# Weight blocks of the first expert stage loaded ahead into the places of S5 tables

## What is computed

```python
for g in range(MOE_GROUPS):                      # 4 groups of 8 experts
    sl = slice(g * MOE_EXPERTS_PER_GROUP, (g + 1) * MOE_EXPERTS_PER_GROUP)
    hg = jnp.einsum('nd,edf->nef', x, w_gate[sl])
    hu = jnp.einsum('nd,edf->nef', x, w_up[sl])
    act = (jax.nn.silu(hg.astype(f32)) * hu.astype(f32)) * combine[:, sl, None]
    y = y + jnp.einsum('nef,efd->nd', act.astype(x.dtype), w_down[sl]).astype(f32)
```

## Time and profile before

| | us |
|---|---|
| median of 3 runs | 1056.37 |
| lowest, highest | 1055.56, 1063.42 |
| profiled execution | 1059.69 |
| its span, first to last instruction | 1057.8 |
| busy: PE, DVE, ACT, POOL | 948.3, 415.3, 197.0, 380.3 |
| mean granted TensorE clock | 0.97 of full |

### The profile page before, as it was taken

One profiled execution on the slowest core, in us unless ns is written; L12 is line 12 of the kernel. 1 busy time (PEld: TensorE's weight loads), 2 busy tenths in 40 slices (PEclk: granted clock), 3 DMA queues, 4 the chain that ended last, 5 costly groups with the idle time before them and its releaser, 6 DMA issues.

```text
span 1057.8 us, 15969 instructions
## 1 busy us (share of the span) xinstructions
PE 948.3 (90%) x5788; PEld 578.5 (55%) x5788; DVE 415.3 (39%) x918; ACT 197.0 (19%) x386; POOL 380.3 (36%) x650
## 2 busy tenths in 40 slices
PE   4999989999988878888799699999999999777896
PEld 4888878655554444444444585444456555434452
DVE  4500245686643223132227781132465233221226
ACT  5423231322300000000025531002441000000012
POOL 1278920193266666666662640000021211101000
PEclk9999999999999999899999899999989999999999
DMA  7127870651779999999983955721067999999964
GB/s 252 41 80 284 305 285 3 262 188 41 278 301 410 419 421 426 422 410 391 389 310 135 154 132 247 317 106 73 20 252 284 421 422 427 422 424 425 422 249 194
DMA packets 45924, 292.06 MB, mean 276 GB/s; under 512 B 10737, under 2 KB 12017, under 8 KB 26391
## 3 DMA queue, kind: packets, MB, share of 16 engines
q1 hardware_dynamic: 35463, 269.92, 64.8%
q0 software_dynamic: 8640, 16.03, 4.1%
q10 hardware_dynamic: 1760, 5.31, 1.7%
HBM read 270.10 MB, written 36.80 MB: 290 GB/s over the span
## 4 chain that ended last, share of the span: by engine, by line
PE 56%; DMA 24%; DVE 6%; SPq 4%; POOL 4%; issue 4%; ACT 1%; POOLq 1%; DVEq 0%; ACTq 0%
PE ps L769 13%; DMA arena<-in_w_gu 11%; PE ps L912 10%; PE ps L1069 10%; DMA arena<-in_w_down 8%; PE ps L1302 5%; PE ps L1055 3%; POOL arena L2461 3%; PE ps L986 2%; SPq L586 2%; DMA arena<-scratch_yd 2%; DVE arena L1706 2%; SPq L582 2%; PE ps L731 2%; PE ps L942 1%
## 5 line engine op out<-in xcount | busy, mean ns | idle before, releaser
L1069 PE MATMUL ps<-arena 128*64 128x256 f32 x2048 | 247.6, 400 | 38.3 <-DMA arena<-in_w_gu 38.3
L1069 PEld LDWEIGHTS ps<-arena 128*64 128x64 f32 x2048 | 154.1, 144 | 131.3 <-DMA arena<-in_w_gu 42.3
L2362 POOL TENSOR_TENSOR arena<-arena 128x32 f32<-128x32 f32 (+5 forms) x233 | 119.0, 511 | 154.6 <-DMA arena<-in_s_d 68.3
L2461 POOL TENSOR_TENSOR arena<-arena 128x256 f32<-128x256 f32 (+3 forms) x192 | 132.1, 688 | 40.5 <-POOL arena L2461 40.0
L769 PE MATMUL ps<-arena 128*128 128x256 f32 (+1 forms) x640 | 142.1, 383 | 0.3 <-ACT arena L1414 0.3
L769 PEld LDWEIGHTS ps<-arena 128*128 128x128 f32 x640 | 121.0, 190 | 19.1 <-ACT arena L1414 0.5
L1055 PE MATMUL ps<-arena 128*64 128x512 f32 x512 | 119.0, 605 | 12.2 <-DMA arena<-in_w_down 11.3
L2109 DVE TENSOR_TENSOR arena<-arena,ps 128x128 f32<-128x128 f32 x64 | 18.4, 287 | 249.0 <-ACT arena L1557 248.9
L912 PE MATMUL ps<-arena 128*128 128x512 f32 x256 | 114.6, 597 | 1.1 <-DMA arena<-in_w_out 1.0
L1557 ACT ACTIVATE arena<-ps 128x128 f32<-128x128 f32 x64 | 17.8, 278 | 460.2 <-PE ps L1069 460.2
L912 PEld LDWEIGHTS ps<-arena 128*128 128x128 f32 x256 | 47.0, 190 | 55.2 <-issue 52.9
(11 more groups left out here) (231 smaller groups left out, 1001.5 us busy)
## 6 DMA issues: line engine op xcount, KB each, us to landing
arena<-in_w_gu SPq DMA_DIRECT2D x64, 2048.0 KB, 14.0
arena<-in_w_down SPq DMA_DIRECT2D x64, 1024.0 KB, 14.0
arena<-in_w_in SPq DMA_DIRECT2D x10, 1024.0 KB, 6.4
scratch_yd<-arena SPq DMA_DIRECT2D x2, 4160.0 KB, 17.7
arena<-scratch_yd SPq DMA_DIRECT2D x16, 512.0 KB, 7.7
arena<-in_w_out SPq DMA_DIRECT2D x1, 4096.0 KB, 12.5
scratch_hd<-arena ACTq DMA_DIRECT2D x8, 512.0 KB
arena<-in_w_glu SPq DMA_DIRECT2D x2, 2048.0 KB, 7.8
```

What stands on the lines that cost most here:

```text
L1069: mm = pe.matmul(ps[CAP * f:CAP * f + CAP, 2 + s, 0:256], XT[l][:, kc, CAP * s:CAP * s + CAP], w[:, kc, 256 * f:256 * f + 256], start=kc = ...
L2362: step(g_.tensor_tensor(out, a, b, op))
L2461: g_.tensor_tensor(o, x, y, f).then_inc(sem("matrix_steps"), 1)
```

## The change

- New places: `EARLY_GU` (two gate-up blocks, at A+38824 and A+34728) and `EARLY_WD` (two sets of down blocks, at A+30632 and A+26536). They lie where GR, GI and M stand later.
- Before `experts(0)` SyncE loads eight blocks ahead or earlier than before: expert 1's gate-up behind the S5 loads; pair 0's down blocks once GpSimd has B-bar and the sample's states are stored; experts 2 and 3 once the sample's output is mixed; expert 5 and pair 2's down blocks behind `x_mixed`; pair 1's down blocks behind the last router product and `h_out`.
- In the stage the early places are filled a second time, for pairs 3 and 4. From pair 5 on the order is that of before.
- There is no S5 build in pairs 0 to 5, 14 and 15. In pairs 6 to 13 two builds are done per pair. V's part (12 tensor_tensor of 256 elements per pair) moves to VectorE (`inputs_of`), ahead of its other work of the pair; GpSimd keeps GR's and GI's (12 operations of 288 elements). TensorE does eight transposes per pair in two groups, VectorE two copies.
- Places that overlapped the new ones move (CS, DB, one of HB). The load of CS also waits for `pool_mixed`. Several semaphores are merged into others.

```diff
+        EARLY_GU = [place(A + at, KC, 512) for at in (38824, 34728)]
+        EARLY_WD = [[place(A + at + 2048 * b, 4, 512) for b in range(2)] for at in (30632, 26536)]
...
             load(DSK, T["s5_d"], "s5_in")
+            def early_gate_up(e, c):
+                sp.dma_start(EARLY_GU[c], T["w_gu"][0][e]).then_inc(sem(f"early_gu_{c}"), 16)
+
+            def early_down(p, c, b):
+                sp.dma_start(EARLY_WD[c][b], T["w_down"][0][b][p]).then_inc(sem(f"early_wd_{c}"), 16)
+
+            sp.wait_ge(sem("stored"), 16 * 4)
+            early_gate_up(1, 0)
             sp.wait_ge(sem("mlstm_parts"), 3)
...
+                    if l == 0 and isinstance(r, int):
+                        sp.wait_ge(sem("gu_done_0"), 1)
+                        load_first(0, 4, 0)
+                        for p in (0, 1):
+                            sp.wait_ge(sem("gu_done_0"), 2 * p + 2)
+                            early_gate_up(2 * p + 7, p)
+                            for b in range(2):
+                                sp.wait_ge(sem("down_done_0"), 2 * p + b + 1)
+                                early_down(p + 3, p, b)
+                            sp.wait_ge(sem("gu_done_0"), 2 * p + 3)
+                            load_first(0, 2 * p + 6, 1 - p)
+                        sp.wait_ge(sem("gu_done_0"), 6)
+                        load_gate_up(0, 11, 0, 1)
+                        for b in range(2):
+                            sp.wait_ge(sem("down_done_0"), 4 + b + 1)
+                            load_down(0, 5, 0, b)
+                        for p in (3, 4):
+                            sp.wait_ge(sem("gu_done_0"), 2 * p + 1)
+                            load_first(0, 2 * p + 4, p % 2)
+                        pair(5, 0, 1)
+                        with sp.Fori(3, 7) as k:
+                            for half in range(2):
+                                pair(2 * k + half, 0, half)
+                        pair(EP - 2, 0, 0, first=False)
...
+            sp.wait_ge(sem("s5_by_pool"), 2)
+            sp.wait_ge(sem("stored"), 16 * 7)
+            for b in range(2):
+                early_down(0, 0, b)
+            sp.wait_ge(sem("mlstm_parts"), 4)
+            load_first(0, 2, 1)
+            early_gate_up(3, 1)
             sp.wait_ge(sem("x_mixed"), 1)
+            load_gate_up(0, 5, 0, 1)
+            for b in range(2):
+                load_down(0, 2, 0, b)
             for n in range(2):
                 load(CIN[n], T["s5_cb"][n], "s5_in")
+            sp.wait_ge(sem("routed"), routed(0, "lg", 4))
+            sp.wait_ge(sem("h_out"), 80)
+            for b in range(2):
+                early_down(1, 1, b)
             experts(0)
...
+                    def inputs_of(p, h):
+
+                        q = 2 * p - 12 + h
+                        two = bass.ds(4 * p - 24 + 2 * h, 2)
+                        br_, bi_ = (a_[:, two].unsqueeze(2).broadcast_to((P, 2, L, CW)) for a_ in (BBR, BBI))
+                        pr_, pi_ = spread(BACKR[:, two], CW), spread(BACKI[:, two], CW)
+                        dve.wait_ge(sem("s5_by_pool"), 3)
+                        dve.wait_ge(sem("m_turned"), q + 1)
+                        done = 0
+                        for out, other, op in ((VR[h], (br_, bi_), ALU.subtract), (VI[h], (bi_, br_), ALU.add)):
+                            for o, x, y, f in ((out, pr_, other[0], ALU.mult), (VTMP, pi_, other[1], ALU.mult),
+                                               (out, out, VTMP, op)):
+                                done += 1
+                                v.tensor_tensor(o, x, y, f).then_inc(sem("v_steps"), 1)
+                                dve.wait_ge(sem("v_steps"), 6 * q + done)
+                        dve.sem_inc(sem("v_ready"), 1)
...
-                    pr_, pi_ = spread(BACKR[:, two], CW), spread(BACKI[:, two], CW)
-                    br_, bi_ = by_step(BBR, L), by_step(BBI, L)
-                    pool.wait_ge(sem("m_turned"), t + 1)
-                    pool.sem_inc(sem("marks"), 1)
-                    mul_add(VR[half], pr_, br_, pi_, bi_, ALU.subtract, GTMP[:, :, 0:L])
-                    mul_add(VI[half], pr_, bi_, pi_, br_, ALU.add, GTMP[:, :, 0:L])
-                    pool.sem_inc(sem("v_ready"), 1)
+                    pool.sem_inc(sem("g_ready"), 1)
```

More of the change, by code:

```diff
@@ L677, in _ @@
             ring.wait_full(sp, "zs", 1)
+            sp.wait_ge(sem("turns_in"), 16)
             load_turns(1)
@@ L1097, in turns @@
                     if l == 0:
-                        with pe.Fori(0, EP // 2 - 1) as k:
-                            for half in range(2):
-                                pair(2 * k + half, half, 0, 2 * k + half, turn=half, k=k)
+                        if isinstance(r, int):
+                            for p in range(6):
+                                pair(p, p % 2, 0, p, turn=p % 2, k=p // 2)
+                            with pe.Fori(3, 7) as k:
+                                for half in range(2):
+                                    pair(2 * k + half, half, 0, 2 * k + half, turn=half, k=k, build=True)
+                        else:
+                            with pe.Fori(0, EP // 2 - 1) as k:
+                                for half in range(2):
+                                    pair(2 * k + half, half, 0, 2 * k + half, turn=half, k=k)
                         if isinstance(r, int):
@@ L2103, in turns, with pair @@
                         lists_again(r)
-                    def pair(p, k, half, follows, last=False):
+                    def inputs_of(p, h):
[13 more added lines that the diff above has]
+                        dve.sem_inc(sem("v_ready"), 1)
+                    def pair(p, k, half, follows, last=False, build=False):
                         n = 2 * p + E * r
+                        if build:
+                            for h in range(2):
+                                inputs_of(p, h)
                         for s in range(2):
@@ L2149, in turns @@
                         ts(RK, RK, -float(CAP), None, ALU.add)
-                    for half in range(2):
-                        pair(half, 0, half, True)
-                    with dve.Fori(1, E // 4 - 1) as k:
+                    if l == 0 and isinstance(r, int):
+                        for p in range(6):
+                            pair(p, p // 2, p % 2, True)
+                        with dve.Fori(3, E // 4 - 1) as k:
+                            for half in range(2):
+                                pair(2 * k + half, k, half, True, build=True)
+                    else:
                         for half in range(2):
-                            pair(2 * k + half, k, half, True)
+                            pair(half, 0, half, True)
+                        with dve.Fori(1, E // 4 - 1) as k:
+                            for half in range(2):
+                                pair(2 * k + half, k, half, True)
                     if isinstance(r, int):
@@ L2510, in scatter, with build @@
                                               ).then_inc(sem(f"y_out_{l}_{half}"), 16)
-                    def build(p, half):
-                        if l == 0 and isinstance(r, int):
-                            matrices(p, half, p)
+                    def build(p):
+                        for h in range(2):
+                            matrices(2 * p - 12 + h)
                     if not isinstance(r, int):
@@ L2528, in turns @@
                         most_rows = pool.value_load(most[0:1, l:l + 1], min_val=0, max_val=NT)
-                    with pool.Fori(0, EP // 2 - 2) as k:
-                        for p, half in ((2 * k + 1, 1), (2 * k + 2, 0)):
-                            scatter(p - 1, 1 - half)
-                            gather(p + 2, half)
-                            build(p, half)
-                    scatter(EP - 4, 0)
-                    gather(EP - 1, 1)
-                    build(EP - 3, 1)
+                    if l == 0 and isinstance(r, int):
+                        for p in range(1, 6):
+                            scatter(p - 1, (p - 1) % 2)
+                            gather(p + 2, p % 2)
+                        with pool.Fori(3, EP // 2 - 2) as k:
+                            for half in range(2):
+                                p = 2 * k + half
+                                scatter(p - 1, 1 - half)
+                                gather(p + 2, half)
+                                build(p)
+                        scatter(EP - 5, 1)
+                        gather(EP - 2, 0)
+                        build(EP - 4)
+                        scatter(EP - 4, 0)
+                        gather(EP - 1, 1)
+                        build(EP - 3)
+                    else:
+                        with pool.Fori(0, EP // 2 - 2) as k:
+                            for p, half in ((2 * k + 1, 1), (2 * k + 2, 0)):
+                                scatter(p - 1, 1 - half)
+                                gather(p + 2, half)
```

(4 more changed lines are left out.)

156 lines of the change are left out of this document (91 added, 65 removed).

## The result

The changed kernel takes 1042.62 us (median of 4 runs, 1039.97 to 1043.31), the kernel before beside it 1057.94 (4 runs): a ratio of 0.9839, with a 95% interval of 0.9806 to 0.9871. Timed again it gave 0.983 [0.9795, 0.9865]. The forecast was 1037.2, in a range of 1029 to 1049.

A forecast was written before the change was run, and what follows sets the result against it. It took layer 0's experts to be bound by DMA bytes. Terms 20.2 + 1.0 - 1 - 1 gave 19.2 us off a median of 1056.4, so 1037.2, in a range of 1029 to 1049.

The forecast's parts named there:

- What bounds the stage: Layer 0's experts cost what their bytes cost: 16.4 us per pair at 416 GB/s; TensorE alone would need 12.0.
- the bytes ahead: Ahead of layer 0's experts, 8.39 MB more is loaded in a hole of the DMA: 20.2 us won.
- rival 3: Early loads issued only near 270, so only the hole from 290 to 297 is filled: 1050 us; chance 0.07.
- The dip near 350: After the early places' last issue the DMA may run dry for 0 to 2 us; taken as -1.
- VectorE's operations: In pairs 6 to 13, twelve of 0.42 us, 0.3 more for six meeting GpSimd: 7.3 us per pair.
- rival 1: VectorE and GpSimd in lock-step, 1.2 us per operation, 38 us lost in pairs 6 to 13: 1075 us; chance 0.07.
- The cover of 0.79 us per operation: In pairs 6 to 13, VectorE's twelve operations cost nothing up to 0.79 us each: (16.7 - 7.2) / 12.
- Theory A: Expectation for 14 VectorE operations: changed kernel at the knee, 18.9 to 19.3 us per pair, 10 to 16 us slower.
- what might get through: In pairs 6 to 13, waits for VectorE that reach the DMA's order, taken as -1 us.
- The tail: End of the stage, pairs 14 and 15 and the reads of stored rows: 0 to 1 us, taken as 0.
- the starting value: Whole kernel before the change: median 1056.4 us, from which the forecast subtracted its sum.

The follow-up runs named there:

- The loads put off: Changed kernel with all early loads issued only once x is mixed, near 270 us: 1053.72 us, 13.2 above the changed kernel beside it.
- the second profile: For the changed kernel: it was run again with no edit, 1040.53 us, stage 229.3 us.
- operations of 512: Changed kernel with VectorE's 12 build operations of 256 elements per pair merged to 6 of 512: 1042.5 us, ratio 0.9837 to the kernel before.
- the two kernels with more operations: Changed kernel with VectorE's build multiplications done twice over, for 12 operations per pair: 20 took 1096.37 us, 14 took 1061.15 us.
- VectorE's third: Changed kernel with VectorE doing 4 of its 12 build operations per pair, tables wrong: 1039.82 us, ratio 0.9832 to the kernel before.
- the filled wait: Changed kernel with 24 extra matmuls ahead of TensorE's wait for the first stored rows behind the stage: 1042.41 us, ratio 0.9852.

## Why the prediction was right

**What bounds the stage, and the bytes ahead: held.** Two profiles of each kernel give 249.1 and 248.6 us before, 230.05 and 229.3 after: 19.05 and 19.3 us for a sum of 19.2. That they agree so closely is chance, since the stages in the table above differ by 3 us. Of the things named ahead, the DMA engines are busy for 0.61 x 6 + 10.3 + 3.8 = 17.8 us from 236 to 262 (15 were expected by 256), the first five pairs are 12.0 apart (six were expected), the waits for weights begin with pair 5 (6 or 7), and the mean period from pair 5 to pair 13 is 17.1 in the one profile and 16.6 in the other (16.4 to 17). The last gate-up block is issued at 516.96, 16 us earlier than before (20 were expected). The loads put off gave 11 us back, and without them the kernel takes what rival 3 says of a head start that isn't had: 5.4 us won by the ratio, 6 in the rival.

**The dip near 350: 0 to 4 us for 1.** In the first profile the DMA share is 1.01 from 340 to 360 and 0.98 from 360 to 380. In the second it is 0.92 and 0.89, 3.8 us less than full, and pair 5 comes 4.4 us later.

**VectorE's operations: held, and a little low.** Predicted 0.42 us alone and 0.3 more for the half that meets GpSimd. The timeline of DVE in the changed kernel's first profile, for the build between pairs 9 and 10 (start, us, idle before):

```profile
439.92 0.42 DVE L2205 TENSOR_TENSOR arena<-arena 128x256 f32 x1
440.53 2.30 DVE L2205 TENSOR_TENSOR arena<-arena 128x256 f32 x5 [0.18 <-DVE arena L2205]
443.31 0.42 DVE L2205 TENSOR_TENSOR arena<-arena 128x256 f32 x1 [0.48 <-DVE arena L2205]
443.92 4.37 DVE L2205 TENSOR_TENSOR arena<-arena 128x256 f32 x5 [0.18 <-DVE arena L2205]
448.52 0.48 DVE L2216 TENSOR_TENSOR arena<-arena,ps 128x128 f32<-128x128 f32 x2 [0.23 <-DVE arena L2205]
```

The first five take 2.30 us, 0.46 each with their gaps; the last five 4.37, 0.87 each. The meeting costs 0.4 us an operation, for 0.3 predicted. As the second half begins, so does GpSimd's first product of the pair:

```profile
443.46 0.80 POOL L2577 TENSOR_TENSOR arena<-arena  x1
```

The build takes 8.4 us here and 7.9 at the same place of the second profile, for 7.3 in the sum. GpSimd's own mean is what it was the earlier trace rows:

```profile
L2577 POOL TENSOR_TENSOR arena<-arena 128x288 f32 x48 | 35.3, 735 | 10.3 <-POOL arena L2577 10.3
```

So rival 1, the lock-step, had no ground. The Trainium skill, "SBUF — State Buffer", section "Who interferes with whom", says that of two such instructions the one that has the port makes the other wait. The trace agrees in that VectorE loses 0.4 us to one of GpSimd's. In the stage no run shows that GpSimd loses as much: its mean rises by only 0.08 us beside operations of 512. Ahead of the stage it lost 2.5 us to one of 4096.

**The cover of 0.79 us per operation: right at one clock only.** This is the step that the forecast got through by luck. In the second profile it is as reckoned: the second block ends at 444.83, the copies end 7.1 us later (7.2 predicted), the build at 459.71, 14.9 us behind the block (14.5 predicted). But once TensorE has waited for VectorE, it is no longer the same TensorE. Pair 10 of the first profile, timeline of PE:

```profile
448.87 0.47 PE L1095 MATMUL ps<-arena 128*128 128x128 f32 x1 [2.87 <-DVE arena L2216]
449.13 1.06 PE L1071 MATMUL ps<-arena 128*128 128x128 f32 x4
...
451.19 4.08 PE L1123 MATMUL ps<-arena 128*64 128x512 f32 x16
```

and the same work in the second profile:

```profile
444.76 0.33 PE L1095 MATMUL ps<-arena 128*128 128x128 f32 x1
444.93 0.60 PE L1071 MATMUL ps<-arena 128*128 128x128 f32 x4
...
446.24 3.65 PE L1123 MATMUL ps<-arena 128*64 128x512 f32 x16
```

The windows of the first profile, across the wait and behind it, show the granted clock in the third column from the right:

```profile
446.00:448.80 2.80, 0.00 (x0) 0.00 (x0) 2.50 (x5) 0.28 (x1) 2.16 (x4) 0.98 0.98 413
448.80:452.00 3.20, 3.13 (x12) 2.29 (x14) 2.04 (x6) 0.00 (x0) 2.18 (x4) 0.50 1.03 429
```

Behind 2.8 us without a matmul the granted clock is 0.50, that is 1.2 GHz. VectorE needs the transposes and down products of this slow stretch before it can start the next build. From the end of one build (448.29) to the start of the next (457.23) it takes 8.9 us. At full clock it takes 7.1: in the second profile 6.7 from VectorE's second multiplication to the build (445.19 to 451.85), and 0.4 ahead of it. A pair in which VectorE is late thus takes 8.9 us plus the build, 17.3 with the 8.4 above (17.5 and 17.6 measured around it), and the threshold is by this estimate (16.7 - 8.9) / 12 = 0.65 us per operation, not 0.79. The 12 operations take 0.70 each. That is why one kernel shows two lists of waits: once VectorE is late, it stays late until the builds end. It became so at pair 9. The second block of pair 8 came late and its products ran at half clock too (6.66 us for 3.67), and the next pair's second block was there soon behind it. Between the two pairs' hidden products lay 14.2 us, where VectorE needed 7.1 + 8.7.

It also fits the two kernels with more operations. With 14 the build is 9.95 us: at full clock 17.1, already over 16.7, and then, behind longer waits, 9.7 + 9.95 = 19.6 (timeline of DVE, 435.01 to 444.71 between the builds):

```profile
425.05 0.88 DVE L2206 TENSOR_TENSOR arena<-arena 128x256 f32 x2
426.10 2.26 DVE L2206 TENSOR_TENSOR arena<-arena 128x256 f32 x5 [0.18 <-DVE arena L2206]
428.98 1.81 DVE L2206 TENSOR_TENSOR arena<-arena 128x256 f32 x2 [0.62 <-DVE arena L2206]
430.98 4.03 DVE L2206 TENSOR_TENSOR arena<-arena 128x256 f32 x5 [0.18 <-DVE arena L2206]
...
444.71 0.42 DVE L2206 TENSOR_TENSOR arena<-arena 128x256 f32 x1
```

With 20 the build takes 14.7 and the way between 9.1: 23.8, where 24 was measured. Theory A's line ran from 17.5 to 24.0, both measured at the low clock, and missed the period by little: with 14 operations the pairs from 6 to 13 were 19.6 us apart on average, for 18.9 to 19.3. Its 10 to 16 us fit a loss counted from 17.5 in eight pairs. Counted from the 16.7 of the DMA engines it is 7 x (19.6 - 16.7) = 20 us, and 19.5 to 20.2 were measured; with 20 operations 7 x (24.2 - 16.7) = 53 for 55. That the clock is the cause of the longer way was read from rows; a kernel that keeps TensorE busy in that wait wasn't run.

By the same count five late pairs cost the changed kernel some 4 us, 4 or 5 x (17.7 - 16.7). The table above has room for that: from pair 5 to pair 14 the first profile took 2.4 to 5.1 us longer than the profiles with VectorE in time. The prediction held this for covered up to 0.79 us per operation and took 1 us for what might get through. It went unseen in the length of the stage because the dip near 350, costed at 1, cost this profile little. That is luck, and the state in which VectorE stays late is what the prediction lacks.

**The tail, costed at 0: it costs 1.8 to 2.0 us.** This is the term that was mis-sized, and the largest part of what the forecast missed. From the last down product to the first S5 product it was 21.6 us in both profiles of the kernel before, and it is 23.4 and 23.6 now (23.3 to 23.6 in the edited kernels but VectorE's third and those with the filled wait). Before, TensorE had the last transposes of the build there (timeline of PE; L1123 multiplies the first stored rows):

```profile
551.55 0.66 PE L1089 MATMUL ps<-arena 128*128 128x128 f32 x4 [0.80 <-POOLq L2481]
552.34 1.95 PE L1123 MATMUL ps<-arena 128*128 128x512 f32 x4
```

In the changed kernel, where L1208 is that line:

```profile
536.55 2.90 PE L1208 MATMUL ps<-arena 128*128 128x512 f32 x4 [2.60 <-DMA arena<-scratch_yd]
539.25 2.68 PE L1215 MATMUL ps<-arena 128*128 128x512 f32 x4
```

The last pair's weights are there in time now, so its products end closer behind the scatter of pair 14, 2.4 us instead of 3.5 behind its landing, and the read of the stored rows can't start before that landing. (The scatter is issued at 523.95 and takes 7.6 us; before.) TensorE waits 2.6 us for it, and the four matmuls behind the wait take 2.90 us for 1.95. It is the longer wait that goes with the lower clock here, and not the missing transposes as such: without them the kernel before would have had 1.60 us between its last down product (to 550.74) and its stored rows. The kernel with VectorE's third waited 1.94 us at this place, kept its clock (1.96 us) and needed 21.4 us for the whole way. With the wait filled, the timeline shows:

```profile
527.42 5.62 PE L1221 MATMUL ps<-arena 128*128 128x128 f32 x48
532.88 1.88 PE L1208 MATMUL ps<-arena 128*128 128x512 f32 x4
```

The clock is full behind it, as expected, but the 24 products run as 48 matmuls and take 5.6 us, twice what I meant, and the way is 24.4 us long. What a filling of the right length gives wasn't tried.

**The sum.** Span, first profiles: stage 19.05, start -2.3, tail -1.8, from the first S5 product to the end 2.0 (485.5 and 483.5): 16.9 us. Second profiles: 19.3 + 0.2 - 2.0 - 1.7 = 15.8. The last piece has the same work in all kernels and lies between 483.5 and 491.6 us in 14 profiles, so its part is variation. The rest of the miss is the starting value: the kernel before has a median nearer 1058 than the 1056.4 of the three runs shown. 1058 - 19.2 + 1.9 = 1040.7, between the two medians of 1042.6 and 1040.5.

## What to carry to other kernels

Where a stage is bound by its bytes, count the idle time of the DMA engines up to the moment at which the first buffer empties: that is what a head start can fill, and half of the early loads did here what all did, as far as can be told. When work is moved to an engine that TensorE waits for, work its threshold out at half TensorE's clock too, since a first late wait lengthens the way to the next. Compare two profiles pair by pair before calling a wait free: two stages of one length can have lost their time in different places. And where a stage is made to end sooner behind a transfer, see what the next one then waits for.

## What the runs showed of the hardware

- VectorE's operation with both inputs in SBUF (256 elements, 0.42 us) takes 0.63 to 1.01 beside GpSimd's products, while the mean of theirs (288 elements) stays at 0.735; beside operations of 512 it is 0.81.
- The granted clock was 0.50 behind TensorE's 2.87 us wait for VectorE, and the four matmuls behind waits of 2.4 to 3.1 us for stored rows took 2.4 to 3.5 us for 1.95; behind one of 1.94 us they did not, nor did the gate-up product behind a wait of 3.3 us for weights in the second profile (3.67 us for 32 matmuls; behind one of the same length in the first it took 6.66).
- A block of 2 MB issued 3.7 us behind a small load on the same queue lengthened VectorE's wait for that load by about 1 us.
